# Three reorderings in the first half of a one-core decoder layer: weight loads, prompt transposes, and the transposes and stores of the K and V rows

## What is computed

```python
q, k, v, bg, u = mixer_inputs(x, g_mix, w_in)         # RMSNorm, one projection 1024 -> 6 x 512
attn = stick_breaking(q, k, v)                        # 8 heads of 64; sample: + 4096 cached tokens,
                                                      #   32 pages of 128 tokens per sequence
c = bg * causal_conv3(u)                              # short gated convolution
h = x + concat(rmsnorm(attn), rmsnorm(c)) @ w_out
h = h + cross_attention(rmsnorm(h), mk, mv)           # 4 heads of 128, 256 memory tokens
h = h + swiglu(rmsnorm(h))                            # width 2816
y = rmsnorm(h)
```

## Time and profile before

| | us |
|---|---|
| median of 3 executions | 1191.43 (1190.54 to 1193.67) |
| profiled execution, its own time | 1196.76 |
| span of its trace | 1195.0 |
| PE busy (matmuls) | 1066.1, 89% |
| DVE busy | 665.4, 56% |
| POOL busy | 409.5, 34% |
| ACT busy | 320.7, 27% |
| moved by DMA | 221.16 MB |

### The profile page before, as it was taken

The page is one execution under the profiler, slowest core; times in us unless marked ns, Lnnn a source line. Parts: engine busy times, 40 slices in busy tenths (PEclk is TensorE's granted clock), DMA queues, the critical chain, the costliest instruction groups (busy, mean ns, idle before and its releaser), DMA issues.

```text
span 1195.0 us, 28991 instructions
## 1 busy us (share of the span) xinstructions
PE 1066.1 (89%) x11527; PEld 913.7 (76%) x11527; DVE 665.4 (56%) x909; ACT 320.7 (27%) x486; POOL 409.5 (34%) x341
## 2 busy tenths in 40 slices
PE   5987999999678879787699889899999999999997
PEld 3765887866435545555599759899999999999996
DVE  2834566758478778563588348655543013544543
ACT  3511112222233524232423252412111112112121
POOL 0515354443323334344333013334333333433330
PEclk9988999999889889998799999899999999999999
DMA  9959687878999999784561132232222222231222
GB/s 352 333 167 328 203 296 245 285 268 273 392 337 329 326 325 318 277 325 146 194 227 37 40 118 91 71 106 70 82 76 72 87 94 82 72 103 44 67 66 80
DMA packets 126501, 221.16 MB, mean 185 GB/s; under 512 B 9951, under 2 KB 68580, under 8 KB 126388
## 3 DMA queue, kind: packets, MB, share of 16 engines
q1 hardware_dynamic: 103234, 146.63, 36.5%
q0 software_dynamic: 20480, 67.13, 15.9%
q10 hardware_dynamic: 2674, 5.87, 1.3%
HBM read 213.78 MB, written 5.80 MB: 184 GB/s over the span
## 4 chain that ended last, share of the span: by engine, by line
PE 66%; DVE 12%; DMA 8%; issue 5%; SPq 4%; ACT 2%; POOL 1%; POOLq 1%; DVEq 0%; ACTq 0%
PE ps L523 38%; PE ps L1664 11%; PE ps L1767 7%; DMA k_set<-in_cache_sb_k 4%; DMA mw_raw<-in_w_in 3%; DVE k_set L1342 2%; PE ps L1818 2%; SPq L618 2%; PE ps L584 2%; SPq L619 2%; DVE r_sq L699 2%; DVE r_sum L704 1%; DVE om_s L1361 1%; PE ps L367 1%; DVE h_lo L428 1%
## 5 line engine op out<-in xcount | busy, mean ns | idle before, releaser
L479 POOL TENSOR_TENSOR w_lo<-w_raw,w_hi 128x2048 fp32r<-128x2048 f32 (+3 forms) x49 | 192.9, 3939 | 404.2 <-ACT w_hi L456 363.6
L523 PE MATMUL ps<-h_hi,w_hi 128*128 128x288 f32 x832 | 180.5, 299 | 8.7 <-DVE h_lo L428 5.7
L523 PE MATMUL ps<-h_lo,w_hi 128*128 128x288 f32 x832 | 179.5, 298 | 0.0
L523 PE MATMUL ps<-h_hi,w_lo 128*128 128x288 f32 x832 | 179.5, 297 | 0.0
L1767 PE MATMUL ps<-k_set,q_blk 32*32 32x256 f32 x4096 | 135.2, 405 | 37.9 <-DVE k_set L1342 19.1
L1342 DVE STREAM_TRANSPOSE k_set<-k_set 128x1024 f32<-128x1024 f32 x128 | 149.7, 1218 | 30.2 <-DMA k_set<-in_cache_sb_k 29.5
L456 ACT ACTIVATE w_hi<-w_raw 128x2048 fp32r<-128x2048 f32 (+3 forms) x47 | 77.9, 1660 | 258.2 <-PE ps L523 228.6
L523 PEld LDWEIGHTS ps<-h_hi,w_hi 128*128 128x128 f32 x832 | 135.6, 191 | 9.7 <-issue 7.2
L1767 PEld LDWEIGHTS ps<-k_set,q_blk 32*32 32x32 f32 x4096 | 79.4, 111 | 77.7 <-issue 34.0
L970 POOL TENSOR_TENSOR mw_lo<-mw_raw,mw_hi 128x1024 fp32r<-128x1024 f32 x32 | 79.2, 2477 | 169.6 <-ACT mw_hi L1040 169.5
L523 PEld LDWEIGHTS ps<-h_lo,w_hi 128*128 128x128 f32 x832 | 135.5, 191 | 0.0
(11 more groups left out here) (266 smaller groups left out, 1684.8 us busy)
## 6 DMA issues: line engine op xcount, KB each, us to landing
k_set<-in_cache_sb_k SPq DMA_DIRECT2D x256, 256.0 KB, 4.8
v_late<-in_cache_sb_v POOLq DMA_DIRECT2D x152, 256.0 KB, 5.8
v_early<-in_cache_sb_v POOLq DMA_DIRECT2D x96, 256.0 KB, 5.1
mw_raw<-in_w_in SPq DMA_DIRECT2D x12, 1024.0 KB, 8.1
w_raw<-in_w_gate SPq DMA_DIRECT2D x11, 1024.0 KB, 5.3
w_raw<-in_w_up SPq DMA_DIRECT2D x11, 1024.0 KB, 5.3
w_raw<-in_w_down SPq DMA_DIRECT2D x8, 768.0 KB, 4.3
w_raw<-in_w_down SPq DMA_DIRECT2D x8, 640.0 KB, 4.0
```

Of the source, the lines that this page charges most:

```text
L479: return nc.gpsimd.tensor_tensor(w_lo[s][:, ks, :], w_raw[s][:, ks, :], w_hi[s][:, ks, :].bitcast(F32), ALU.subtract)
L523: op = nc.tensor.matmul(ps[:, 2 * t + hf, 0:b - a], weights[s][:, k, t * P:(t + 1) * P], x[:, k0 + k, a:b], start=begin and k == ks[0] and ...
```

## The change

In the order of the diff's parts:

- **Slot before pages.** In SP's iterations 1 to 10 `load_tiles(C + 1)` stands ahead of `k_half(C + 2)`. Tile 3 stands ahead of the weight transposes of chunk 0 on PE.
- **Memory slots.** Slots 12 and 13 (w_ck) are asked for in iterations 17 and 20 and no longer in 12 and 13, slots 14 and 15 (w_cv) in 23 and 26 (24 and 27 before). The memory tiles are in chunks 21 to 23 and 25 to 29.
- **K rows, V rows.** The four items of the K rows move from chunk 11 to chunk 30, which now also has the two of mv that chunk 31 had. The V rows are stored in chunk 28, the K rows in chunk 30 (both in chunk 12 before). `k_rows` lies in another place.
- **Prompt transposes first.** In a page chunk `prompt_transposes` is the first work on PE (it stood behind `half_scores(C + 2, 0)`, the items of part 0 and the tile), and ACT's copy of them stands ahead of its item copies.
- **Last V pages.** POOL asks for the last eight V pages in its iteration 29, ahead of pages 244 to 247; before, they came behind these.
- **Queries.** In chunks 13 and 21 DVE does two K block transposes and the evacuation ahead of `queries`.

```diff
--- before.py
+++ after.py
@@ -115,7 +115,7 @@
         mv_tok = at("mv_tok", [MT, CH], R_K + 4096)
         mk_rows = at("mk_rows", [MT, CH], R_M + 1024)
         v_tok = at("v_tok", [5, CH], R_V)
-        k_rows = at("k_rows", [NB, CH], R_H + 24576)
+        k_rows = at("k_rows", [NB, CH], R_M + 5120)
 
 
         T_Q, T_K, T_A, T_B, T_C, T_U = 0, 4, 8, 12, 16, 20
@@ -315,9 +315,10 @@
         I_CS = [([cs[:, j, :] for j in range(4)], cs_rows)]
 
         SPARE = (6, 2 * P)
-        ITEMS = {LAST - 1: list(zip(I_K, ((5, 0), (7, 0)) * 2)), LAST: list(zip(I_V, ((5, 0), (7, 0)) * 2))}
+        ITEMS = {LAST: list(zip(I_V, ((5, 0), (7, 0)) * 2))}
         ITEMS.update({C: [(item, SPARE) for item in I_M[2 * i:2 * i + 2]] for i, C in enumerate((15, 17, 18, 19))})
-        ITEMS.update({CHUNKS - 2: list(zip(I_MK + I_CS, ((1, 0), (2, 0), (3, 0)))), CHUNKS - 1: list(zip(I_MV, ((1, 0), (2, 0))))})
+        ITEMS[CHUNKS - 2] = list(zip(I_MK + I_CS + I_K[0:2] + I_MV + I_K[2:4],
+                                     ((1, 0), (2, 0), (3, 0), (5, 0), (7, 0), (1, 0), (2, 0), (5, 0), (7, 0))))
         FIRST_ITEM = {C: sum(len(v) for k, v in ITEMS.items() if k < C) for C in range(CHUNKS + 1)}
 
         def items_of(C, part):
@@ -338,7 +339,7 @@
             _, _, kind, k = SLOTS[j // 2]
             return kind, k + j % 2
 
-        MEM_TILES = {C: TILES + i for i, C in enumerate((22, 23, 25, 26, 27, 28, 29, 30))}
+        MEM_TILES = {C: TILES + i for i, C in enumerate((21, 22, 23, 25, 26, 27, 28, 29))}
 
         def v_place(n):
             if n >= 8 * (CHUNKS - 1):
@@ -632,7 +633,7 @@
 
         def sums_at(C):
 
-            return o_sum[(C >= LAST) + (C >= 24) + (C >= CHUNKS - 2)][:, :, :]
+            return o_sum[(C >= LAST) + (C >= 24) + (C >= CHUNKS - 3)][:, :, :]
 
         def step_of(U):
 
@@ -934,12 +935,12 @@
                     sp.wait_ge(m_["rows"], LAST + 1)
                     sp.wait_ge(m_["half"], 16)
                     sp.dma_start(m_row[:, :, :], mem[0].rearrange("(m p) n -> p m n", p=P)).then_inc(s_mrow, 16)
+                if 2 <= C + 1 < TILES // 2:
+                    load_tiles(C + 1)
                 if C + 2 < CHUNKS:
                     k_half(sp, C + 2)
-                if 2 <= C + 1 < TILES // 2 or C + 1 in (13, 14):
-                    load_tiles(C + 1 if C < 12 else C)
-                if C in (24, 27):
-                    load_tiles(14 + (C - 24) // 3)
+                if C in (17, 20, 23, 26):
+                    load_tiles(12 + (C - 17) // 3)
             sp.wait_ge(s_gt, TILES + 8)
             load_stage(sp, "out")
 
@@ -947,6 +948,7 @@
                 return sp.dma_start(place[:, :, :], src[0, b].rearrange("(m p) h d -> p m (h d)", p=P))
             sp.wait_ge(s_op["out"], KD)
             sp.wait_ge(s_out, 16 * 4)
+            sp.wait_ge(s_kv_out, 16 * 4)
             for b in range(BS):
                 load_mem(cmk, b, smk_tok[b]).then_inc(s_cmk, 16)
             load_stage(sp, "cq")
@@ -985,10 +987,14 @@
                     tile_lo(2 * C + 4)
                 if C + 1 in MEM_TILES:
                     tile_lo(MEM_TILES[C + 1])
-                v_pages(pool, range(8 * C + RING, min(8 * C + RING + 4, 8 * CHUNKS)))
+                if C == CHUNKS - 3:
+                    v_pages(pool, range(8 * CHUNKS - 8, 8 * CHUNKS))
+                if C < CHUNKS - 2:
+                    v_pages(pool, range(8 * C + RING, 8 * C + RING + 4))
                 if 2 * C + 5 < TILES:
                     tile_lo(2 * C + 5)
-                v_pages(pool, range(8 * C + RING + 4, min(8 * C + RING + 8, 8 * CHUNKS)))
+                if C < CHUNKS - 3:
+                    v_pages(pool, range(8 * C + RING + 4, 8 * C + RING + 8))
             for name in NAMES[NAMES.index("out"):]:
                 lo_stage(pool, name)
 
@@ -1043,8 +1049,8 @@
             def copy_items(C, part):
                 for n, _, (srcs, dst), (bank, c0) in items_of(C, part):
                     f = srcs[0].shape[-1]
-                    if C == CHUNKS - 1:
-                        act.wait_ge(m_["rows"], C)
+                    if n == FIRST_ITEM[CHUNKS] - 4:
+                        act.wait_ge(m_["rows"], CHUNKS - 2)
                     act.wait_ge(s_it, n + 1)
                     nc.scalar.activation(dst, tiled(ps[0:f, bank, c0:c0 + len(srcs) * P]), ACT.Copy).then_inc(s_ic, 1)
 
@@ -1115,13 +1121,15 @@
                 rms_root(act, "conv", rstd_c[:, :], T, CH, 0)
                 nc.scalar.preload_act_table(ACT.Sigmoid)
 
-            def store_k_v():
-                act.wait_ge(s_ic, FIRST_ITEM[LAST + 1])
+            def store_v():
                 act.dma_start(out_v_p[0, 0].rearrange("(m p) h d -> p m (h d)", p=P), v_tok[:, 0:NB, :]).then_inc(s_kv_out, 16)
+
+            def store_k():
+                act.wait_ge(s_ic, FIRST_ITEM[CHUNKS])
                 act.dma_start(out_k_p[0, 0].rearrange("(m p) h d -> p m (h d)", p=P), k_rows[:, :, :]).then_inc(s_kv_out, 16)
 
             def store_memory_k():
-                act.wait_ge(s_ic, FIRST_ITEM[CHUNKS - 1])
+                act.wait_ge(s_ic, FIRST_ITEM[CHUNKS - 2] + MT)
                 act.dma_start(out_mk[0, 0].rearrange("(m p) h d -> p m (h d)", p=P), mk_rows[:, :, :]).then_inc(s_out, 16)
 
             def store_memory_v():
@@ -1137,11 +1145,11 @@
                         tile_hi(2 * C + 3)
                     if 3 <= u < 19:
                         prompt_out(u - 3)
+                    if 2 <= u < 18:
+                        copy_prompt_weights(u - 2)
                     copy_items(C, 0)
                     if C == 10:
                         conv_root()
-                    if 2 <= u < 18:
-                        copy_prompt_weights(u - 2)
                     if c == 0 and g:
                         copy_new_weights(g)
                     copy_items(C, 1)
@@ -1158,16 +1166,16 @@
                         prompt_sigmoids(u)
                     if C == 8:
                         conv_squares()
-                    if C == LAST:
-                        store_k_v()
+                    if C == CHUNKS - 4:
+                        store_v()
                     if C == 19:
-                        act.wait_ge(s_kv_out, 16 * 4)
                         act.wait_ge(s_ic, FIRST_ITEM[20])
                         hi_parts(act, "ck", mT, G_MEM, range(KD))
                     if C == CHUNKS - 2:
                         store_memory_k()
+                        store_memory_v()
+                        store_k()
                 if last:
-                    store_memory_v()
                     act.wait_ge(s_vsum, 8 * CHUNKS - 10)
                     hi_parts(act, "out", pT[:, T_C:T_C + KC, :], None, range(KC))
 
@@ -1468,12 +1476,14 @@
                     sample_rows(g)
                 if 1 <= u < 17:
                     prompt_weights(u - 1)
-                if c == 5 and g < GROUPS - 1:
-                    queries(g + 1)
-                if more:
+                turn = c == 5 and g < GROUPS - 1
+                if more and not turn:
                     k_blocks(C + 3, range(2))
                 if C in MEM_TILES:
                     evac(MEM_TILES[C])
+                if turn:
+                    queries(g + 1)
+                    k_blocks(C + 3, range(2))
                 if more:
                     k_blocks(C + 3, range(2, 4))
                 if C == 20:
@@ -1671,12 +1681,12 @@
                         pe.wait_ge(s_ic, n)
                         if bank == 6:
                             pe.wait_ge(m_["rows"], C)
-                        if C == LAST - 1:
+                        if C == LAST:
                             pe.wait_ge(s_gf, TILES)
                         if C == 15:
                             pe.wait_ge(s_mrow, 16)
-                    elif part:
-                        pe.wait_ge(s_ic, n - (1 if bank == 6 else 2) + 1)
+                    elif part or i >= 5:
+                        pe.wait_ge(s_ic, n + 1 - (4 if C == CHUNKS - 2 else 1 if bank == 6 else 2))
                     for j, src in enumerate(srcs):
                         f = src.shape[-1]
                         op = nc.tensor.transpose(ps[0:f, bank, c0 + j * P:c0 + (j + 1) * P], src, ident)
@@ -1841,11 +1851,11 @@
                     tile(2 * C + 2)
                 if c == 0 and g:
                     sample_rows(g)
+                if C == 0:
+                    tile(3)
                 weight_transposes(C)
                 if C == 10:
                     pe.wait_ge(s_rt["conv"], 1)
-                if C == 0:
-                    tile(3)
                 half_scores(C + 2, 0)
                 half_scores(C + 2, 1)
                 if c == 0 and g:
@@ -1863,6 +1873,8 @@
                 u, ahead = C - LAST, C + 2 < CHUNKS
                 if c % 2 == 0:
                     banks_read(C)
+                if 2 <= u < 18:
+                    prompt_transposes(u - 2)
                 if ahead:
                     half_scores(C + 2, 0)
```

(4 more changed lines are left out.)

## The result

| | before | after |
|---|---|---|
| median, us | 1191.94 (1190.54 to 1193.67, 4 executions) | 1175.56 (1172.46 to 1179.88, 4 executions) |
| profiled execution, its own time | 1196.76 | 1176.88 |
| span of its trace | 1195.0 | 1175.1 |

The ratio is 0.9864 (95% interval 0.9828 to 0.9900): 16.2 us faster, 12 to 20.5. The forecast was 26.9 us faster, 1164.5; the time is in the wide range (1150 to 1179), outside the forecast's own (1157 to 1172), and within 1 us of the front-only rival (1176.5). The profiled execution of the kernel before took about 5 us more than the median, that of the kernel after about 1 us more, so differences between the two traces run 3 to 4 us above those between the medians.

The account below looks back on a forecast made before the run. PE bound 116 to 282 us, DMA 295 to 352, a page loop 352 to 553. Terms 14.9 + 9 + 1.5 - 5 + 8.5 - 2 + 0 = 26.9 us: median 1164.5, range 1150 to 1179.

Parts of the forecast that it names:

- front-only rival: After the first half, freed DMA time is paid back and the loop's pace stays; only Term 1: 1176.5 us, chance 0.22.
- Term 1: Up to half 4: slot before pages and tile 3 early remove PE's stall near 107 us, 14.9 us faster.
- K pages late: Chunks 2 to 10: DVE's wait for K pages takes the stall's place, 1198 us, chance 0.05.
- Term 2: Full stretch, 295 to 352 us: four 1 MB transfers leave, 9 us faster; K items leaving chunk 11 give 1.5 more.
- Term 3: Stretch from 352 us: slots 12 and 13 come back there, 5 us slower.
- Term 4: Page chunks: prompt transposes first shorten DVE's 32.1 us of waits for them, 8.5 us faster.
- Term 5: Chunk 21: one memory tile moves there from chunk 30, 2 us slower.
- Term 6: End of the pages, chunks 30 and 31: no change, 0 us, bounds -3 and +4.

Follow-up runs that it names:

- the front alone: Kernel before with slots ahead of K pages in iterations 1 to 10 and tile 3 ahead of the weight transposes: 11.1 us faster (7.9 to 14.3).
- all but the front: Changed kernel with SP's old order in iterations 1 to 10 and tile 3 in its old place: 3.9 us faster than the kernel before.

## Why the prediction was right or wrong

The direction was right, and the largest term with it. The sum was not: 26.9 us were forecast and 16.2 came. That the time lies in the range is owed to the range's width, which the front-only rival had set.

**Term 1** was right in place and size in the trace: -16.2 for -14.9 to half 4 (15.0 in the mean of thirteen traces), by both of its steps (tile 3: 4.7 said, 4.8 found; tile 6 at 103.4 said, 102.3 found; the slower clock's 2.4 us came back). In time the front alone gave 11.1, so 15 is above what can be shown.

**K pages late**, the slower rival, did not happen. Between 110 and 266 us no wait of DVE for K pages is listed. But the pages do land later. The K pages of this stage, kernel before (116 to 282 us) and after (110 to 266 us):

```profile
k_set<-in_cache_sb_k SPq DMA_DIRECT2D x64, 256.0 KB, 4.5
k_set<-in_cache_sb_k SPq DMA_DIRECT2D x65, 256.0 KB, 5.2
```

In the kernel before, the first of the eight pages of a half lands in 2.4 to 3.2 us; behind a slot, issued 1.15 us earlier, in 4.6 to 5.4. By the Trainium skill, "DMA: Bandwidth & Descriptors", "Queues, rings and completion order", each DMA engine consumes the descriptors of a ring in order, and the estimate from it was up to 20 us lost. The trace fits the order (a mere sharing of the engines with the slot is not told apart here), and not the loss: the pages had the slack that the prediction worked out. Those of half 6 have landed by 135.3 and DVE turns to them at 139.85, 4.5 us later, where 4.0 was said. Behind slot 12, at a share of 1.03 (340 to 365 us), the pages take 9.0 to 13.4 us; there DVE has no slack and waits the 7.63 us above.

**Term 2 failed**, and it is the step that the forecast fell by: 3.3 us where it said 9. It took four transfers at the stretch's rate. First, the stretch moved only 1.9 MB less (56.9 us at 361 GB/s, 53.5 at 349), and not 4.2, in part because the V pages' ring took four more pages and because slot 12, issued at 290.89 and landed at 301.4, had been in it only from 295.2 on. Second, 1.9 MB at 361 GB/s are 5.2 us and 3.3 came, as the rate fell to 349. That rate was no limit of the DMA engines, since the same stretch moves 376 GB/s with the slots put back. Each half of the term holds by itself (stores away: 3.4 in the stretch, 5.5 in all; slots away: 3.7), which together would be 7.1. All of it away, with the K items gone and the transposes first, gives 3.3, 3.9 (V pages in the old order) and 6.4 (all but the front). Why the last, which has the same code in these chunks, is 3 us shorter is open. So a DMA share of 0.98 does not show that bytes set the pace when something that loads ahead (the V pages' ring) fills what is free. That the remaining floor is the loop from half to issue, landing, transpose and half is supported by the trace with the page numbers read ahead (49.0), and not proven by its time.

**Terms 3 to 5** came to +1.4 for -1.5 together. Term 3 was about right in size: with the slots early again the two stretches behind the full one are 5.8 us shorter than in the changed kernel (5 said); the three other pairs have 2.7, 9.3 and, the other way, 0.4, so one pair of traces doesn't fix it, and in time the late slots cost 0.6 and 2.2 us, both inside the intervals. Term 4 was mis-sized: 3.9 us for 8.5. I had seen that DVE's wait for PE hides a wait for K pages in some chunks, and yet counted chunk by chunk what each would give; the wait for pages rose by 17 of the 32 us. And PE's new wait for ACT, which I had put at no more than 1 us a place and inside the 6, sums to 6.9 us in nine places, the longest 1.2. How much of it costs time is not shown. Term 5: the tile costs 1.1 us, with an interval (1.7 faster to 3.8 slower) that tells neither from 0 nor from the 2 said.

**Term 6** was put at 0, and the traces say 3 to 4 us lost to that order of the pages. I had noted that the missing pages would be those of chunk 30, and balanced it with a last page that goes out some 2 us earlier. It goes out 15.4 us after half 31 where it was 16.0, so 0.6 of the 2 came. Against the kernel before, the changed kernel's last stretch is 1.3 us longer.

**The rivals.** Front only was the nearest in time, at a chance of 0.22, though "all but the front" is not quite nothing (3.9, 0.7 to 7.2). It was nearest by luck in part: its reason, that the loop's pace does not change, does not fit the full stretch, which did get shorter (3.3 to 6.4 us) and was partly lost again by the slots and the page order.

**A reading.** The DMA rate falls to about 70 GB/s from the twenty-second slice on and not from the twentieth, which still has 194; nothing was built on it.

## What to carry to other kernels

A stall of PE whose chain runs back through one engine's queue to a load that was asked for late can be counted from the rows: the place and the 15 us at that place came out to within 1 or 2 us, though 11 (7.9 to 14.3) are what the time shows. A gain from taking bytes out of a full stretch should be counted only up to what the next bound allows: look whether a ring that is loaded ahead will take the room, at the round trip of the load that is really waited for, and at the rate beside the share. When two orders of the same transfers are at hand, put first the ones needed first. And a wait taken from an engine in a loop can turn up as the next wait on the same engine, as 17 of 32 us did here.

## What the runs showed of the hardware that was not expected

Eight page loads take SP 8.1 us, of which only half is the issue: with the page numbers read ahead they take 4.0 us. A page load issued 1.15 us behind a 1 MB load of the same queue landed about 2 us later than one without it (4.6 to 5.4 for 2.4 to 3.2 us, the first page of a half, at a DMA share of 0.80), and in 9.0 us behind slot 12, at a share of 1.03; a reader with 4 us of slack did not notice the first. The share of 0.98 stood beside 349 GB/s in one kernel and 1.03 beside 376 in another, for the same stretch of work. Executions of one kernel spread by up to 13 us here (1184.0 to 1197.4 for the kernel before), more than most of these edits are worth, so that single traces could only place the changes and not weigh them.
